# Modulation rows on GpSimd: 48 instead of 32 in each second-table stage, none in the sliding attention and the mixing stage

## The chip, the cores and the metric

The kernel runs on one core of a Trainium2 chip. The metric is the time of one execution on the device in microseconds (us). The engines are named as the profile names them: PE is TensorE (PEld its weight loads), DVE is VectorE, ACT is ScalarE, POOL is GpSimd, SP the engine whose queue issues nearly all loads here.

## What is computed

Three transformer-like layers on 256 tokens of width 1024, in float32. The first has gated linear attention, the second sliding-window attention with a shared key and value; each is followed by a retrieval over 16384 single-neuron experts. The third has retention beside latent attention (the mixing stage) and a mixture of 32 experts. Every norm is scaled and shifted by a modulation vector, and every residual is gated by one. These vectors depend only on the conditioning inputs `c` and `c_2`, not on the tokens, so their products can be computed at any time before they are used:

```python
mod = c_act @ mod_w[l] + mod_b[l]                       # D -> 6 D, also kv_mod and the third layer's
sh1, sc1, g1, sh2, sc2, g2 = jnp.split(mod, 6, axis=-1)
h = modulate(x, norm_g[l, 0], sh1, sc1)
x = x + (g1[:, None, :] * mixer(h)).astype(x.dtype)

def peer(h, w_q, subkeys, u_tab, v_tab):                # per head: two top-16, then the best 16 of 256 pairs
    u = u_tab[e]
    a = gelu(einsum('pd,phkd->phk', xb, u))
    return einsum('phk,phkd->pd', g * a, v_tab[e])
```

The kernel computes the retrieval densely: all 16384 rows of the first table (u) and then of the second (v), with a gate that is zero where an expert isn't chosen.

## The kernel before

**Modulation rows.** The modulation vectors have 160 blocks of 128 outputs; the weights of one block are a row of 512 KB in the stream, 128 partitions by 1024 values. The first 16 rows are made at the start. The other 144 go over GpSimd (`mod_pool`, L2499). For each row it waits for the load, multiplies the 1024 values by the activated conditioning (L2505), halves three times by addition (512, 256 and 128 columns: L2507, L2509, L2517) and leaves 128 partial sums per partition in a "part". TensorE then sums the part over the partitions with a matmul of one column (`column`, L773 and L775). Two buffers alternate: row j may be loaded when row j-2 is made (semaphore `mod_made`), and a part is written again when its column is done (`mod_column`).

**Where the rows lie.** `MODS_GLA` gives 40 rows to the first attention and the queries after it, `MODS_DOWN` 32 rows to each of the two second-table stages, `MODS_SWA` 16 to the sliding attention, `MODS_MIX` 16 to the mixing stage and `MODS_MOE` 8 to the last experts. In the sliding attention and the mixing stage the program of SP is written out by hand (`loads_with_mods`, L547): a list `at` says behind which weight slot a modulation load goes. It stands in the same queue as the loads of the ring of four weight slots, and waits there for `mod_made`. Groups of eight columns are taken by `mods_pe` (two groups after the sixth output projection, L1067; one after the retention values and one before the retention scores), and `mods_dve` adds the bias.

**The second-table stage.** `down_pe` (L954) runs over 128 tiles of the table, 16 in a turn of its loop. A tile is 12 matmuls of 512 columns (L973). ScalarE rounds the tile's two halves and the gated activations to their high parts (`down_high`, L1445 and L1453), VectorE subtracts to get the low parts (`down_low`, L2106 twice for the halves, L2109 for `a_parts`). Their program is in the order of tiles, and the order binds them: `a_parts` has two buffers, the table parts eight halves, that is four tiles. ScalarE waits at L1453 for TensorE's matmuls on the tile before last. SP loads eight tiles ahead (`v_used`: low parts of tile c-8 made; four ahead in the first turn). After every fourth table tile SP loads a modulation row into the first half of `hT` or into `mean`; on TensorE the column of a row stands behind tiles 3, 7, 11 and 15 of a turn. The parts lie in `hT`, four of them. All columns go to bank 0, and VectorE takes them together at the end (L2120).

**The sliding attention.** Four key tiles, four value slots, eight query tiles w_q0 to w_q7 (w_q0 and w_q1 as plain float32, L747; the others with weights split by ScalarE, L1292, and VectorE, L1746, L695 on TensorE). Behind w_q3 stand four small matmuls that rotate the keys (L1046), behind w_q7 eight for the queries (L1051). VectorE turns each with L2164, L2166 and L2168. Then come the scores, softmax, weighted values, and the output projection with the square sums of the next norm (L649).

**The mixing stage.** `mix_pe` begins with `ret_q`, `ret_k` (L695) and `ret_v` (L719), all with split weights; between the splits of `ret_k` and `ret_v` VectorE does one step of the rotation per slot (L2220, L2224).

## Time and profile before

| | us |
|---|---|
| median of 3 runs | 3214.8 |
| lowest and highest | 3210.15, 3217.36 |
| the profiled execution | 3215.8 |
| its span, first to last instruction | 3214.0 |

The granted TensorE clock over the profiled span was 0.965 of full speed.

| engine | busy us | share |
|---|---|---|
| PE | 2985.8 | 93% |
| PEld | 2696.5 | 84% |
| DVE | 2045.3 | 64% |
| ACT | 1621.4 | 50% |
| POOL | 1562.5 | 49% |

The two second-table stages run from 786 to 1154 us and from 1886 to 2255 us; the sliding attention follows the first, to about 1340 us, and the mixing stage the second, to about 2625 us. Busy shares over the whole span say little here, as the stages have different limits; each is read in its own window. A group of instructions that overlap is shown as one line with its count: "3.00 ... x2" is the time from the start of the first to the end of the second. An engine's idle time stands in brackets with what ended it.

### The profile page before, as it was taken

Reading aid. Unit: us, or ns where it says so; the run is one execution under the profiler, and the core shown is the slowest. Engines: PE = TensorE matmul, PEld = TensorE weight load, DVE = VectorE, ACT = ScalarE, POOL = GpSimd, SP = SyncE. Lnnn points to the kernel's source line nnn. Section 1 sums busy time; section 2 is a strip of 40 time slices with the busy share of each in tenths; the row PEclk is TensorE's granted clock in tenths of the full one; section 3 lists DMA queues with packets and bytes.
Section 4 is the critical chain, followed back from the end, with each engine's and each line's share of the span. In section 5 each row is a group of like instructions: output and inputs, shape, how many; then the busy total and the mean of one; then the engine's idle time right before and its main releaser. Section 6 shows DMA issues by size and latency. Waiting matters only on the chain.

```text
span 3214.0 us, 57845 instructions
## 1 busy us (share of the span) xinstructions
PE 2985.8 (93%) x18908; PEld 2696.5 (84%) x18908; DVE 2045.3 (64%) x3376; ACT 1621.4 (50%) x3195; POOL 1562.5 (49%) x1229
## 2 busy tenths in 40 slices
PE   7988999987999986999999789999799999999998
PEld 6678999976787875899999677778689789999997
DVE  6647960057888868279300778888784436777776
ACT  1124555578555543355555965555554325555553
POOL 5867898975444436158988645444361010000100
PEclk8989999999999997999999999999999999999998
DMA  6545555521766632345555037665464235555553
GB/s 246 201 148 175 181 181 181 183 72 59 261 230 228 228 134 105 109 159 182 182 182 189 7 131 257 226 229 202 151 216 145 92 125 191 190 194 191 197 194 125
DMA packets 153463, 552.57 MB, mean 172 GB/s; under 512 B 16896, under 2 KB 19712, under 8 KB 153232
## 3 DMA queue, kind: packets, MB, share of 16 engines
q1 hardware_dynamic: 151136, 547.42, 50.2%
q10 hardware_dynamic: 2224, 3.87, 0.4%
q8 instruction: 53, 0.87, 0.1%
q14 instruction: 50, 0.41, 0.0%
HBM read 550.17 MB, written 1.05 MB: 172 GB/s over the span
## 4 chain that ended last, share of the span: by engine, by line
PE 74%; ACT 9%; DVE 6%; issue 6%; POOL 3%; DMA 1%; ACTq 0%; DVEq 0%; SPq 0%; POOLq 0%
PE bank L947 23%; PE bank L973 20%; PE bank L1218 12%; PE bank L747 6%; PE bank L1239 5%; ACT hT L1434 5%; PE bank L695 3%; ACT hT L1430 2%; POOL arena L2505 1%; DVE w_parts L1746 1%; POOL arena L2507 1%; PE bank L649 1%; DMA arena<-stream 1%; POOL arena L2509 1%; DMA ring<-stream 1%
## 5 line engine op out<-in xcount | busy, mean ns | idle before, releaser
L2462 POOL TENSOR_TENSOR w_parts<-ring,w_parts 128x512 fp32r<-128x512 f32 x512 | 661.9, 1300 | 169.9 <-ACT w_parts L1399 119.3
L947 PE MATMUL bank<-h_parts,w_parts 128*128 128x256 f32 x6144 | 738.3, 283 | 5.1 <-POOL w_parts L2462 5.1
L947 PEld LDWEIGHTS bank<-h_parts,w_parts 128*128 128x128 f32 x6144 | 737.5, 191 | 5.5 <-POOL w_parts L2462 5.5
L2505 POOL TENSOR_TENSOR arena<-arena,cact 128x1024 f32<-128x1024 f32 x80 | 168.7, 2109 | 747.2 <-DMA arena<-stream 746.9
L1399 ACT ACTIVATE w_parts<-ring 128x512 fp32r<-128x512 f32 x512 | 322.8, 632 | 318.3 <-PE bank L947 316.4
L1218 PEld LDWEIGHTS bank<-h_parts,w_parts 128*128 128x128 f32 x3072 | 374.6, 193 | 3.8 <-DVE arena L2324 1.5
L1218 PE MATMUL bank<-h_parts,w_parts 128*128 128x256 f32 x3072 | 375.5, 284 | 1.4 <-DVE arena L2324 1.4
L1586 ACT ACTIVATE w_parts<-ring 128x512 fp32r<-128x512 f32 x384 | 241.9, 631 | 266.8 <-PE bank L1218 167.9
L973 PE MATMUL bank<-w_parts,a_parts 128*128 128x512 f32 x1536 | 371.0, 397 | 1.1 <-DVE a_parts L2109 1.1
L973 PE MATMUL bank<-h_parts,a_parts 128*128 128x512 f32 x1536 | 365.4, 393 | 6.1 <-DVE a_parts L2109 6.1
L2393 DVE TENSOR_TENSOR w_parts<-ring,w_parts 128x512 fp32r<-128x512 f32 x376 | 268.9, 727 | 150.3 <-ACT w_parts L1586 147.0
L973 PEld LDWEIGHTS bank<-h_parts,a_parts 128*128 128x128 f32 x1536 | 284.7, 188 | 80.4 <-DVE a_parts L2109 22.4
L973 PEld LDWEIGHTS bank<-w_parts,a_parts 128*128 128x128 f32 x1536 | 286.5, 190 | 60.7 <-DVE a_parts L2109 2.6
L1453 ACT ACTIVATE a_parts<-arena 128x256 fp32r (+1 forms) x256 | 107.1, 418 | 363.6 <-PE bank L973 361.7
L695 PE MATMUL bank<-h_parts,w_parts 128*128 128x256 f32 x1920 | 240.8, 287 | 16.5 <-DVE w_parts L1746 14.7
L695 PEld LDWEIGHTS bank<-h_parts,w_parts 128*128 128x128 f32 x1920 | 236.5, 195 | 20.4 <-issue 17.1
L2109 DVE TENSOR_TENSOR a_parts<-arena,a_parts 128x256 fp32r<-128x256 f32 x256 | 168.7, 659 | 115.6 <-ACT a_parts L1453 115.3
L1746 DVE TENSOR_TENSOR w_parts<-ring,w_parts 128x512 fp32r<-128x512 f32 x184 | 194.0, 1085 | 64.6 <-ACT w_parts L1292 63.2
L921 PE MATMUL bank<-hT,h_parts 128*128 128x128 f32 x1024 | 145.9, 295 | 68.8 <-ACT hT L1434 67.2
L2067 DVE COPY bank<-cst 128x128 f32<-128x128 f32 x2 | 0.6, 294 | 320.4 <-ACT arena L1404 320.4
L921 PEld LDWEIGHTS bank<-hT,h_parts 128*128 128x128 f32 x1024 | 129.1, 202 | 85.7 <-ACT hT L1434 85.6
L1239 PE MATMUL bank<-w_parts,a_parts 128*128 128x512 f32 x768 | 182.8, 394 | 4.9 <-DVE a_parts L2405 4.1
(325 smaller groups left out, 4595.0 us busy)
## 6 DMA issues: line engine op xcount, KB each, us to landing
ring<-stream SPq DMA_DIRECT2D x786, 512.0 KB, 3.4
arena<-stream SPq DMA_DIRECT2D x192, 512.0 KB, 4.3
hT<-stream SPq DMA_DIRECT2D x32, 512.0 KB, 4.6
mean<-stream SPq DMA_DIRECT2D x32, 512.0 KB, 4.5
arena<-consts ACTq DMA_DIRECT2D x1, 1536.0 KB, 6.3
xT<-xin ACTq DMA_DIRECT2D x1, 1024.0 KB, 10.7
out<-hT SPq DMA_DIRECT2D x4, 256.0 KB, 2.2
arena<-subk ACTq DMA_DIRECT2D x2, 128.0 KB, 2.1
```

The costliest lines, as they stand in the source:

```text
L695: mm = pe.matmul(t[:, 0:T], w[:, wp, q * P:(q + 1) * P], h_parts[:, hp, 4 * j + q, :], start=(j == 0 and q == 0 and i == 0), stop=(j == 1 ...
L921: mm = pe.matmul(bank[4 + k][:, (s % 4) * P:(s % 4 + 1) * P], hot2[:, s, :].bitcast(F32), hot1[:, s, :], start=True, stop=True)
L947: mm = pe.matmul(bank[k][:, 0:T], w[:, wp, ws], h_parts[:, hp, 4 * j + q, :], start=(j == 0 and q == 0 and i == 0), stop=(j == 1 and q == ...
L973: mm = pe.matmul(bank[4 + 2 * a + e][:, :], a_parts[:, k % 2, ap, a * P:(a + 1) * P], w[:, wp, :], start=False, stop=False, skip_group_che ...
L1218: mm = pe.matmul(bank[2 * e_par + m][:, f * T:(f + 1) * T], w[:, wp, q * P:(q + 1) * P], h_parts[:, hp, 4 * j + q, :], start=(j == 0 and q ...
L1239: mm = pe.matmul(bank[4 + 2 * a + e][:, :], a_parts[:, ap, f, a * P:(a + 1) * P], w[:, wp, :], start=(f == 0 and i == 0), stop=(f == 1 and ...
L1399: act.activation(w_parts[half % HALVES][:, 0, :], ring[slot_][:, j * 512:(j + 1) * 512], ACT.Copy).then_inc(sem(f"{n}_high"), 1)
L1586: act.activation(w_parts[half % HALVES][:, 0, :], ring[s][:, j * 512:(j + 1) * 512], ACT.Copy).then_inc(sem("e_high"), 1)
L1746: dve.tensor_tensor(w[:, 1, :], slot(name, k)[:, j * 512:(j + 1) * 512], w[:, 0, :].bitcast(F32), ALU.subtract).then_inc(sem("x_low"), 1)
L2393: dve.tensor_tensor(w[:, 1, :], ring[moe_slot(k)[0]][:, j * 512:(j + 1) * 512], w[:, 0, :].bitcast(F32), ALU.subtract).then_inc(sem("e_low ...
L2462: pool.tensor_tensor(w[:, 1, :], ring[(base + k) % RING][:, j * 512:(j + 1) * 512], w[:, 0, :].bitcast(F32), ALU.subtract).then_inc(sem(f" ...
L2505: pool.tensor_tensor(b3, b3, c_b, ALU.mult).then_inc(sem("mod_step"), 1)
```

## The change

The 16 rows of the sliding attention and the 16 of the mixing stage move into the two second-table stages, which get 48 each. Six rows go with a turn of 16 tiles, loaded and summed behind tiles 3, 6, 8, 11, 13 and 15 (`DOWN_AT`). The parts become six, two in each of three chunks of `hT`. The order of rows stays; since the rows of the second layer's stage begin at 104, GpSimd writes its first two turns out (the first eight rows use the first conditioning vector, the others the second) and loops over the rest. The SP programs of the sliding attention and the mixing stage become plain loops over weight slots. `mods_pe` and `mods_dve` are not called there any more.

```diff
-MODS_DOWN = ((56, 88), (104, 136))
-MODS_SWA = (88, 104)
-MODS_MIX = (136, 152)
+MODS_DOWN = ((56, 104), (104, 152))
+DOWN_AT = (3, 6, 8, 11, 13, 15)
+TURN_MODS = len(DOWN_AT)
...
-            return [hT[:, 4 + i, 0:P] for i in range(4)]
+            return [hT[:, 4 + i // 2, i % 2 * P:(i % 2 + 1) * P] for i in range(TURN_MODS)]
...
-                    if c % 4 == 3:
-                        mod_load(seg, seg[0] + c // 4)
+                    if c % 16 in DOWN_AT:
+                        mod_load(seg, seg[0] + c // 16 * TURN_MODS + DOWN_AT.index(c % 16))
...
-                        if c % 4 == 3:
-                            j = j0 + c // 4
-                            sp.wait_ge(sem("mod_made"), it * 4 + (j - 1))
-                            sp.dma_start(mod_buffers(seg)[j % 2], stream[it * 12 + (row0 + 3 * (c // 4))])\
+                        if c % 16 in DOWN_AT:
+                            i = c // 16 * TURN_MODS + DOWN_AT.index(c % 16)
+                            j = j0 + i
+                            sp.wait_ge(sem("mod_made"), it * TURN_MODS + (j - 1))
+                            sp.dma_start(mod_buffers(seg)[j % 2], stream[it * 3 * TURN_MODS + (row0 + 3 * i)])\
                               .then_inc(mod_landed[j % 2], 16)
...
-            at = [kv + 3 * i // 2 for i in range(10)] + [MO["swa_out"][0] + 2] * 4 + [MO["swa_out"][0] + 4, MO["swa_out"][0] + 5]
-            loads_with_mods(kv, MO["peer1_q"][0], MODS_SWA, MODS_SWA[0], at)
+            loads(kv, MO["peer1_q"][0])
...
-            loads_with_mods(mix, MO["mix_out"][1], MODS_MIX, MODS_MIX[0], [mix + 5 * i // 2 for i in range(16)])
+            loads(mix, MO["mix_out"][1])
...
-                    if k % 4 == 3:
-                        m = k // 4
-
-                        pe.wait_ge(sem("mod_made"), it * 4 + (mod_number(MODS_DOWN[l][0]) + m + 1))
-                        column(pe, bank[0][:, bass.ds(it * 4 + m, 1)], mod_parts(MODS_DOWN[l])[m]).then_inc(sem("mod_column"), 1)
+                    if k in DOWN_AT:
+                        m = DOWN_AT.index(k)
+
+                        pe.wait_ge(sem("mod_made"), it * TURN_MODS + (mod_number(MODS_DOWN[l][0]) + m + 1))
+                        column(pe, bank[0][:, bass.ds(it * TURN_MODS + m, 1)], mod_parts(MODS_DOWN[l])[m]).then_inc(sem("mod_column"), 1)
...
-            project_norm(pe, "swa_out", A.o, "w_out", "1b", between={5: lambda: [mods_pe(pe, MODS_SWA, g) for g in (11, 12)]})
+            project_norm(pe, "swa_out", A.o, "w_out", "1b")
...
-            mods_pe(pe, MODS_MIX, 17)
...
-            mods_pe(pe, MODS_MIX, 18)
...
-            for lo, hi, c in ((0, 2, c_b), (2, 8, c2_b if l else c_b)):
-                with pool.Fori(0, hi - lo) as it:
-                    for i in range(4):
-                        j = j0 + 4 * lo + i
-                        mod_pool(pool, seg, i, j, c, it)
+            turns = NK // 16
+            first = 2 if l else 0
+
+            for m in range(first * TURN_MODS):
+                mod_pool(pool, seg, m, j0 + m, c_b if m < 8 else c2_b)
+            with pool.Fori(0, turns - first) as it:
+                for i in range(TURN_MODS):
+                    mod_pool(pool, seg, i, j0 + first * TURN_MODS + i, c2_b if l else c_b, it)
...
-            mods_pool(pool, MODS_SWA, 0)
             peer_pool(pool, 1)
-            mods_pool(pool, MODS_MIX, 1)
```

## Rows read from the trace of the kernel before

**Rows 1.** The page, part 2: busy tenths of GpSimd in 40 slices.
```profile
POOL 5867898975444436158988645444361010000100
```

**Rows 2.** Chain that ended last, in second-table stages: start us, us, what.
```profile
799.70 0.11 PE bank L775 x2
...
810.95 11.02 PE bank L973 x48
...
1921.75 11.03 PE bank L973 x48
...
1957.60 11.22 PE bank L973 x48
...
2243.69 11.02 PE bank L973 x48
```

**Rows 3.** Stage window: length; PE, PEld, DVE, ACT, POOL busy; clock, DMA share, GB/s.
```profile
1957.60:2254.80 297.20, 294.70 (x1302) 238.25 (x1302) 250.89 (x307) 150.20 (x307) 130.34 (x100) 1.00 0.63 219
```

**Rows 4.** Timeline of GpSimd in second-table stages: start us, us, instruction, idle before.
```profile
786.62 1.90 POOL L2505 TENSOR_TENSOR hT<-hT,cact 128x1024 f32<-128x1024 f32 x1 [11.20 <-DMA hT<-stream]
...
790.84 0.46 POOL L2517 TENSOR_TENSOR hT<-hT 128x128 f32<-128x128 f32 x1 [0.17 <-POOL hT L2509]
...
1934.25 2.08 POOL L2505 TENSOR_TENSOR hT<-hT,cact 128x1024 f32<-128x1024 f32 x1 [5.11 <-DMA hT<-stream]
...
1940.92 2.09 POOL L2505 TENSOR_TENSOR mean<-mean,cact 128x1024 f32<-128x1024 f32 x1 [1.15 <-DMA mean<-stream]
```

**Rows 5.** Timeline of VectorE in second-table stages.
```profile
974.97 0.78 DVE L2109 TENSOR_TENSOR a_parts<-arena,a_parts 128x256 fp32r<-128x256 f32 x1 [1.26 <-ACT a_parts L1453]
...
978.52 0.68 DVE L2109 TENSOR_TENSOR a_parts<-arena,a_parts 128x256 fp32r<-128x256 f32 x1
...
1933.88 3.00 DVE L2106 TENSOR_TENSOR h_parts<-arena,h_parts 128x512 fp32r<-128x512 f32 x2
1936.80 1.51 DVE L2109 TENSOR_TENSOR a_parts<-arena,a_parts 128x256 fp32r<-128x256 f32 x1
...
1940.24 0.41 DVE L2109 TENSOR_TENSOR a_parts<-arena,a_parts 128x256 fp32r<-128x256 f32 x1
1940.58 2.98 DVE L2106 TENSOR_TENSOR w_parts<-ring,w_parts 128x512 fp32r<-128x512 f32 x2
...
1953.92 1.28 DVE L2106 TENSOR_TENSOR w_parts<-arena,w_parts 128x512 fp32r<-128x512 f32 x2
```

**Rows 6.** Timeline of SP's queue and of ScalarE in the sliding attention.
```profile
1207.72 0.33 SPq L545 DMA_DIRECT2D arena<-stream  x1
...
1212.49 0.63 ACT L1292 ACTIVATE w_parts<-ring 128x512 fp32r<-128x512 f32 x1 [4.77 <-DMA ring<-stream]
```

**Rows 7.** Timeline of TensorE in the sliding attention.
```profile
1197.88 7.07 PE L747 MATMUL bank<-arena,ring 128*128 128x256 f32 x32
...
1318.91 3.62 PE L747 MATMUL bank<-arena,ring 128*128 128x256 f32 x16
1322.36 1.84 PE L775 MATMUL bank<-cst,arena 128*128 128x1 f32 x16
...
1326.81 5.30 PE L747 MATMUL bank<-arena,ring 128*128 128x256 f32 x16
```

**Rows 8.** Timeline of VectorE in the sliding attention, a rotation's first and last step.
```profile
1257.81 0.42 DVE L2164 TENSOR_TENSOR arena<-bank,rope_s 128x256 f32<-128x256 f32 x1
...
1258.73 0.56 DVE L2168 TENSOR_TENSOR arena<-arena 128x256 f32<-128x256 f32 x1
```

**Rows 9.** Mixing stage: one window (columns as in rows 3), then TensorE's timeline.
```profile
2289.70:2365.10 75.40, 64.85 (x436) 58.48 (x434) 69.16 (x55) 34.72 (x62) 52.69 (x35) 1.00 0.65 218
...
2337.71 11.13 PE L719 MATMUL bank<-w_parts,h_parts 128*128 128x512 f32 x48 [0.93 <-DVE w_parts L1746]
...
2365.07 1.84 PE L775 MATMUL bank<-cst,arena 128*128 128x1 f32 x16
...
2367.03 42.04 PE L695 MATMUL bank<-h_parts,w_parts 128*128 128x256 f32 x336
```

## What the change should do to the time

> **What bounds the kernel now.** I read the page's slices first, then the second-table stages (786 to 1154 us and 1886 to 2255 us), then the two stages that lose work. [rows 1] are GpSimd's slices: 4 or 5 tenths in the two second-table stages (digits 11 to 14 and 25 to 28), and again right after each of them, in the sliding attention and in the mixing stage. In the second-table stage the chain of waits is nearly all matmuls of L973: 48 of them, four tiles, take 11.02 us, and 11.22 where something held them up [rows 2]. So a tile costs TensorE 2.755 us, and a modulation column 0.12 us (0.11 in the row at 799.70). From the group at 1957.60 to the end of the one at 2243.69 run 104 tiles in 297.1 us, which is 45.71 us for a turn of 16. Sixteen clean tiles and four columns would be 44.08 + 0.48 = 44.56, so four modulation rows now cost 1.15 us of stall a turn, 0.29 each.
>
> The stall comes from VectorE. It makes the low parts for the same tiles and is busy 250.9 of 297.2 us there [rows 3]. GpSimd needs 4.68 us for a modulation row while VectorE rests [rows 4]. While both work, VectorE's instructions stretch: a pair of 128x512 subtractions takes 3.00 us against 1.28, an a_parts subtraction 1.51 against 0.41 [rows 5]. Free, a tile costs VectorE 0.34 + 1.28 = 1.62 us. Between 1933.88 and 1953.92 three modulation rows follow each other while VectorE does six tiles, so two tiles take 6.68 us (6.70 from 1933.88 to 1940.58); so a modulation row takes 6.68 - 3.24 = 3.44 us from VectorE. TensorE wants two tiles in 5.57 us (with half a column each): VectorE falls back 1.1 us for each such row, and 0.29 of it shows as stall when it had no lag before. A tile without GpSimd gives back 2.755 - 1.62 = 1.14 us. The check: these three should cost 0.29 + 1.10 + 1.10 = 2.49 us; in the chain the eight tiles from 1932.90 (1921.75 + 11.03 + 0.12) to 1957.60 took 24.70 us against 22.28 clean, 2.42 us lost.
>
> **What the change takes away.** (a) Sliding attention. In the SP queue each modulation load waits for GpSimd, and the ring loads stand behind it: the one at 1207.72 goes out only then, and the ring load behind it lets ScalarE go on at 1212.49, after 4.77 us of idleness [rows 6]. TensorE has no gap until w_q0 and w_q1 are done at about 1205 (1197.88 + 7.07) [rows 7]. Without these loads the ring runs ahead, and six split projections (24 matmuls each, 3.0 us at the rate of 42.04 us for 336 [rows 9]) and four small rotations (an estimate of 1.2 us: 4 x 256 columns, and the waits for their banks) end near 1205 + 18.2 + 1.2 = 1224.5. Then VectorE's eight rotations follow; one takes 1.5 us where GpSimd does not touch it (1257.81 to 1259.30) [rows 8], so they end near 1237 instead of 1259.3: 22 us less. What is late next is TensorE with its projections; between 19 (their clock lower for part of it) and 24 us. (b) The two groups of columns inside the output projection, at 1322.36, hold TensorE for 2 x 1.96 = 3.9 us (1.96 is the group of the mixing stage, below), and the 16 matmuls after them take 5.30 instead of 3.62 us [rows 7]: 5.6 us in sum, 3.9 at least. VectorE's two small additions and the gains lie beside matmuls: nothing. (c) Mixing stage. From 2289.7 to 2365.1, 75.4 us, TensorE does 336 matmuls of 256 columns and 96 of 512. At the rates of stretches without idleness (42.04 us for 336, 11.13 for 48) that is 42.0 + 22.3 = 64.3 us, so 11.1 us are waits for VectorE, which is busy 69 of the 75 us [rows 9]. GpSimd's 35 instructions there are nearly nine modulation rows, 9 x 3.44 = 31 us of VectorE's 69; without them VectorE has 38 us of work in 64. I take 10 us, between 7 and 11. (d) The columns of the two groups there: 2365.07 to 2367.03, 1.96 us, and the same once more, 3.9 us. Sum of what goes: 22 + 5.6 + 10 + 3.9 = 41.5 us, from 33.8 to 44.5. The tiles opened later shift to other banks in the rotation of four; that costs nothing, since the order of openings and evictions stays.
>
> **What it adds.** In each second-table stage 16 more rows: 16 loads of 512 KB, 64 GpSimd instructions, 16 columns. The DMAs: the stage moves 219 GB/s now at a share of 0.63 [rows 3]; 22 loads instead of 20 per turn make that about 0.69, still far from full, so nothing for bandwidth. The wait for the row before last now stands more often in SP's queue; behind it are the table loads. These are issued eight tiles (22 us) ahead of VectorE, and a row needs up to 4.8 us to land [rows 6] and 5.5 us on GpSimd (1934.25 to 1939.77, where its idle time before 1940.92 begins) [rows 4], so the queue has over 10 us to lose first: nothing. TensorE's wait before a column looks for a row loaded some twelve tiles earlier: nothing. The unrolled GpSimd rows of the second layer issue the same instructions. What counts is VectorE's time. Its demand in a turn becomes 16 x 1.62 + 6 x 3.44 = 46.6 us, above TensorE's clean 44.80 (with six columns): VectorE becomes the bound.
>
> The order 3, 6, 8, 11, 13, 15 decides the rest. Rows at 3, 6 and 11 have a free tile before them; each leaves 1.1 - 0.29 = 0.81 us of lag, less than the 1.14 us that a free tile gives back. Rows at 8, 13 and 15 follow two tiles behind another and cost 1.10 each. A turn: 44.80 + 3 x 0.29 + 3 x 1.10 = 48.97 us, 3.26 more than now. Some rows begin while VectorE rests and take only 2.27 us from it (974.97 to 979.20, 4.23 us for work of 1.96) [rows 5]; of the eight in that stretch of 92 us this was one. With them I take +2.9 a turn for the six regular turns of a layer. The first turn has such rows mostly, +1.0. In the second the loads bunch, as they do now (the arena half of the ring opens at once): 0.29 + 5 x 1.10 = 5.8 us against about 2.8 now, +3.2 with the columns. A layer: 1.0 + 3.2 + 6 x 2.9 = 21.6; both: 43 us. Bounds: 0.29 for every row, 46.54 a turn, +0.83 x 16 = 13 us; and every turn as bunched as the second, 44.80 + 5.79 = 50.59, +4.9 x 16 = 78 us. I stay at 43 because both spots with contiguous rows show the full price.
>
> By the Trainium skill ("SBUF — State Buffer", section "Who interferes with whom") a VectorE instruction with two SBUF inputs and a GpSimd instruction that reads SBUF exclude each other for their whole length. The trace agrees in kind, not in full: a row that is 4.68 us long takes 3.44.
>
> **Sum.** The profiled execution has 3215.8 us (span 3214.0), 1.0 above the median of 3214.8. 3215.8 - 41.5 + 43 = 3217.3; for the median 3216.3, I say 3216. Within 0.2% (6.4 us, about what a measurement of this kernel can tell) this is no change: two large sums that cancel.
>
> **The rivals.** *Faster: the added rows hide.* If rows behind another also fall into VectorE's rests, each costs 0.29 and a turn 46.54: 13 us against 41.5, 3186; with half of them 3200. For it: the first turn of the first layer, where the chain shows groups of 11.02 in spite of its rows (810.95) [rows 2]. Against: VectorE has no rests while it lags. *Slower: GpSimd's rows run together in every turn.* Rows at 11, 13, 15 are loaded 5.6 us apart and GpSimd needs 5.5 us for one under contention. If the next row is there when one ends, VectorE never gets its free tile; the turn is 50.6 us, 78 - 41.5 = +36, 3251; if only some turns do so, 3235. It decides once a row waits in its buffer when GpSimd ends the one before, that is where GpSimd's 5.5 us exceed the spacing of the loads; for it the second turns, against it GpSimd's idle 1.15 us even between the contiguous rows [rows 4]. *Slower: the gain is smaller.* If in the attention and mixing stages ScalarE or a lower clock keeps half of the waits (a) and (c), 16 us stay: 3232. *Full exclusion.* If each row took its whole 4.68 us, two tiles would be 7.92 us, the lag per row 2.35, and a turn at least 44.80 + 14.1 - 4.6 = 54.3: +8.6 x 16 = 138, 3312. This is the skill's lock taken strictly; the triple speaks against it.
>
> **How the numbers follow.** Forecast 0.33 (3209 to 3222 on its own), hidden rows 0.28, run-together rows 0.28, smaller gain 0.09, full exclusion 0.02. Faster by over 0.2%: 0.29; within: 0.33; slower: 0.38. The range 3190 to 3246 leaves out the far half of the hidden case, the ends of the run-together case and full exclusion.
>
> **What would show it.** Right: second-table turns near 48.6 us, VectorE busy over 95% of them with little idleness before L2109, GpSimd rows in blocks of one, two and three; the sliding attention's last rotation 22 us earlier after the stage's start; no waits on L1746 in the mixing stage. Wrong: turns below 47 us or above 50; waits for ring loads left in the attention; VectorE's instructions stretched by clearly less than 3.4 us a row in a block.

## The result: 1.5% slower

The changed kernel takes 3259.4 us (median of 4, from 3252.6 to 3269.0), the kernel before 3212.7 beside it: 1.0146 times the time, 95% interval 1.0117 to 1.0175. The forecast of 3216 and its range up to 3246 were too low. The profiled executions took 3258.8 and 3215.8 us, 43.0 apart. One execution of the kernel of the first experiment ran at a granted clock of 0.456 and took 11133.6 us; it is left out of that kernel's numbers. By stages:

```
us                 first table  second table 1  attention  first table 2  second table 2  mixing   experts
before                 482.2        367.2         250.2        482.8          368.0        385.9    535.5
after                  482.4        414.7         220.0        483.3          411.4        366.2    535.1
forecast change          0          +21.6         -27.6          0            +21.6        -13.9      0
measured change        +0.2         +47.5         -30.2        +0.5           +43.4        -19.7    -0.4
```

(A second-table stage and the experts reach from their first matmul to the start of their last; "first table" from its first matmul to the first of the second table; "attention" and "mixing" from the start of the last matmul of a second-table stage to the first of the stage behind.) The saving was 49.9 us instead of 41.5, the cost 90.9 instead of 43. So the gain was found and somewhat larger, and the added rows cost twice what the sum gave them.

The page of the kernel after, GpSimd's, VectorE's and the clock's slices; the second is to be compared with [rows 1]:

```profile
DVE  6647950067998977379300889899664436777776
POOL 5867898865665530058988656565100001000100
PEclk8989999999999998999999999999999999999998
```

GpSimd stands at 5 or 6 tenths in the second-table stages and at 0 to 3 right behind them. The second-table stages in two windows (columns: length; PE, PEld, DVE, ACT, POOL busy; clock, DMA share, GB/s), to compare with [rows 3]:

```profile
787.70:1202.80 415.10, 380.03 (x1634) 303.15 (x1633) 362.29 (x376) 183.82 (x376) 251.44 (x192) 0.98 0.63 221
1905.70:2317.50 411.80, 376.77 (x1633) 301.55 (x1633) 360.25 (x376) 183.71 (x376) 250.40 (x192) 0.99 0.63 222
```

VectorE is busy 87% of the time, not over 95%: it isn't simply full, and it isn't the bound that the forecast made it. Yet TensorE waits for it. The waits in the second of these windows, after (line, what it waited for, us in total, times, longest), then the same stage of the kernel before:

```profile
PE bank L963 <- DVE a_parts L2097: 34.8, 39, 1.8
...
DVE a_parts L2097 <- ACT a_parts L1441: 47.9, 46, 6.2
```

```profile
PE bank L973 <- DVE a_parts L2109: 4.2, 8, 0.9
...
DVE a_parts L2109 <- ACT a_parts L1453: 57.6, 65, 6.2
```

TensorE waits 34.8 us for VectorE (4.2 before), and in the same stage VectorE idles 47.9 us for ScalarE's high parts, which in turn wait until TensorE frees one of the two a_parts buffers. Both happen in turns: VectorE falls back while GpSimd works, catches up, and can't get more than the two buffers ahead.

One regular turn shows it. GpSimd's timeline, the product that begins each row, with its idle time before:

```profile
2103.79 1.90 POOL L2491 TENSOR_TENSOR hT<-hT,cact 128x1024 f32<-128x1024 f32 x1 [8.86 <-DMA hT<-stream]
...
2114.55 2.12 POOL L2491 TENSOR_TENSOR mean<-mean,cact 128x1024 f32<-128x1024 f32 x1 [5.41 <-DMA mean<-stream]
...
2120.08 2.08 POOL L2491 TENSOR_TENSOR hT<-hT,cact 128x1024 f32<-128x1024 f32 x1
...
2130.68 1.90 POOL L2491 TENSOR_TENSOR mean<-mean,cact 128x1024 f32<-128x1024 f32 x1 [5.09 <-DMA mean<-stream]
...
2136.00 2.08 POOL L2491 TENSOR_TENSOR hT<-hT,cact 128x1024 f32<-128x1024 f32 x1
...
2141.47 2.35 POOL L2491 TENSOR_TENSOR mean<-mean,cact 128x1024 f32<-128x1024 f32 x1
```

These are blocks of one, two and three rows, as the forecast had them, but inside a block there is no idle time at all, where [rows 4] had 1.15 us. So it is in 9 of the 12 regular turns: the second row of the pair and both followers in the block of three begin within 0.12 us of the row ahead. VectorE's timeline in the same stretch:

```profile
2129.06 0.43 DVE L2097 TENSOR_TENSOR a_parts<-arena,a_parts 128x256 fp32r<-128x256 f32 x1 [0.78 <-ACT a_parts L1441]
...
2132.03 0.83 DVE L2097 TENSOR_TENSOR a_parts<-arena,a_parts 128x256 fp32r<-128x256 f32 x1 [1.27 <-ACT a_parts L1441]
...
2136.24 4.08 DVE L2094 TENSOR_TENSOR w_parts<-arena,w_parts 128x512 fp32r<-128x512 f32 x2
...
2147.71 0.41 DVE L2097 TENSOR_TENSOR a_parts<-arena,a_parts 128x256 fp32r<-128x256 f32 x1
```

and TensorE's, with the idle time before:

```profile
2103.09 5.97 PE L963 MATMUL bank<-w_parts,a_parts 128*128 128x512 f32 x24
...
2109.48 5.74 PE L963 MATMUL bank<-h_parts,a_parts 128*128 128x512 f32 x24 [0.29 <-DVE a_parts L2097]
...
2120.74 2.88 PE L963 MATMUL bank<-h_parts,a_parts 128*128 128x512 f32 x12
2125.33 3.04 PE L963 MATMUL bank<-h_parts,a_parts 128*128 128x512 f32 x12 [1.70 <-DVE a_parts L2097]
...
2136.76 2.99 PE L963 MATMUL bank<-h_parts,a_parts 128*128 128x512 f32 x12
2141.24 3.02 PE L963 MATMUL bank<-w_parts,a_parts 128*128 128x512 f32 x12 [1.49 <-DVE a_parts L2097]
...
2145.83 3.02 PE L963 MATMUL bank<-w_parts,a_parts 128*128 128x512 f32 x12 [1.46 <-DVE a_parts L2097]
```

VectorE stands idle 0.78 and 1.27 us just ahead of the block of three; then its pair of subtractions takes 4.08 us where 1.28 is the free time, and TensorE waits 1.49 and 1.46 us. From 2132.03 to 2147.71, both the start of an a_parts subtraction, VectorE does four tiles in 15.68 us; TensorE alone needs 11.02.

What each block costs TensorE in this turn can be read from the starts of its tiles, with 2.755 us for a tile and 0.16 for a column, the measured price of one (below). The single row: 6.39 us from 2103.09 to 2109.48 for two tiles and a column, 0.7 lost. The pair: 4.59 us from 2120.74 to 2125.33 for one tile, 1.8 lost. The block of three: 9.07 us from 2136.76 to 2145.83 for two tiles and a column, 3.4 lost. In sum 5.9 us.

Now the stages that lost work. In VectorE's timeline the last rotation of the sliding attention begins 80.3 us after the stage did (1202.8); in [rows 8] it was 104.1 (from 1153.7):

```profile
1283.12 0.42 DVE L2152 TENSOR_TENSOR arena<-bank,rope_s 128x256 f32<-128x256 f32 x1
```

TensorE's output projection has eight pieces of 16 matmuls. After, the first three stand in one row, then the sixth and the eighth (to compare with [rows 7]):

```profile
1325.44 10.60 PE L737 MATMUL bank<-arena,ring 128*128 128x256 f32 x48 [0.57 <-issue]
...
1344.08 3.62 PE L737 MATMUL bank<-arena,ring 128*128 128x256 f32 x16
...
1351.85 3.62 PE L737 MATMUL bank<-arena,ring 128*128 128x256 f32 x16
```

The first three and the eighth before:

```profile
1300.27 10.60 PE L747 MATMUL bank<-arena,ring 128*128 128x256 f32 x48 [0.57 <-issue]
...
1332.39 3.62 PE L747 MATMUL bank<-arena,ring 128*128 128x256 f32 x16
```

And a window of the mixing stage, to compare with [rows 9]:

```profile
2352.71:2455.12 102.41, 102.41 (x769) 98.66 (x769) 63.48 (x86) 60.70 (x107) 0.00 (x0) 1.00 0.55 185
```

In the mixing window TensorE has no gap in 102.41 us; it does 336 + 96 + 336 matmuls there (40.59, 21.95 and 40.47 us in the timeline).

### The profile page after: what moved, and what is told of

Its sections match the earlier page's. It is cut to its first block, busy times and chain, and to the rows that moved or that the text cites. A ratio compares the mean times of both kernels' runs of the same rounds, so it can differ in the third digit from the quotient of the medians.

```text
span 3257.0 us, 58401 instructions
## 1 busy us (share of the span) xinstructions
PE 2991.1 (92%) x18900; PEld 2695.8 (83%) x18900; DVE 2084.7 (64%) x3372; ACT 1621.2 (50%) x3195; POOL 1553.8 (48%) x1229
## 4 chain that ended last, share of the span: by engine, by line
PE 60%; issue 15%; DVE 8%; ACT 8%; POOL 8%; DMA 1%; DVEq 0%; ACTq 0%; POOLq 0%; SPq 0%
PE bank L937 23%; PE bank L1206 11%; PE bank L963 7%; PE bank L1227 5%; PE bank L737 5%; ACT hT L1422 5%; PE bank L685 4%; DVE h_parts L2094 2%; DVE a_parts L2097 2%; DVE w_parts L2094 2%; ACT hT L1418 2%; POOL mean L2491 1%; POOL hT L2491 1%; POOL mean L2493 1%; POOL arena L2491 1%
## 5 line engine op out<-in xcount | busy, mean ns | idle before, releaser
L2446 POOL TENSOR_TENSOR w_parts<-ring,w_parts 128x512 fp32r<-128x512 f32 x512 | 659.7, 1299 | 327.0 <-ACT w_parts L1387 286.1
L963 PE MATMUL bank<-w_parts,a_parts 128*128 128x512 f32 x1536 | 383.3, 404 | 35.3 <-DVE a_parts L2097 35.3
L963 PE MATMUL bank<-h_parts,a_parts 128*128 128x512 f32 x1536 | 376.1, 398 | 34.8 <-DVE a_parts L2097 34.5
L2491 POOL TENSOR_TENSOR arena<-arena,cact 128x1024 f32<-128x1024 f32 x48 | 99.0, 2063 | 566.3 <-DMA arena<-stream 566.2
L2377 DVE TENSOR_TENSOR w_parts<-ring,w_parts 128x512 fp32r<-128x512 f32 x376 | 271.1, 732 | 148.8 <-ACT w_parts L1574 145.5
L2097 DVE TENSOR_TENSOR a_parts<-arena,a_parts 128x256 fp32r<-128x256 f32 x256 | 215.1, 840 | 96.2 <-ACT a_parts L1441 96.1
L1734 DVE TENSOR_TENSOR w_parts<-ring,w_parts 128x512 fp32r<-128x512 f32 x184 | 145.6, 806 | 95.2 <-ACT w_parts L1280 93.7
L2479 POOL TENSOR_TENSOR w_parts<-ring,w_parts 128x512 fp32r<-128x512 f32 x8 | 12.2, 1536 | 381.8 <-ACT w_parts L1574 381.7
```

Source lines behind the costliest of these rows:

```text
L963: mm = pe.matmul(bank[4 + 2 * a + e][:, :], a_parts[:, k % 2, ap, a * P:(a + 1) * P], w[:, wp, :], start=False, stop=False, skip_group_che ...
L2097: dve.tensor_tensor(a_parts[:, k % 2, 1, :], W[:, bass.ds(it * 16 + k, 1), :].rearrange("p i t -> p (i t)"), a_parts[:, k % 2, 0, :].bitca ...
L2377: dve.tensor_tensor(w[:, 1, :], ring[moe_slot(k)[0]][:, j * 512:(j + 1) * 512], w[:, 0, :].bitcast(F32), ALU.subtract).then_inc(sem("e_low ...
L2446: pool.tensor_tensor(w[:, 1, :], ring[(base + k) % RING][:, j * 512:(j + 1) * 512], w[:, 0, :].bitcast(F32), ALU.subtract).then_inc(sem(f" ...
L2491: pool.tensor_tensor(b3, b3, c_b, ALU.mult).then_inc(sem("mod_step"), 1)
```

## The experiments

Every theory below is about one of three things: whether the two sums are independent, what a row on GpSimd takes from VectorE and TensorE, and how this depends on the distance between rows. "Turn" is 16 tiles, measured between every sixteenth a_parts subtraction of VectorE; where one number stands for regular turns it is the mean of turns 3 to 7 of both layers.

### The saving alone

No row in the sliding attention and the mixing stage, and none added elsewhere.

```diff
-MODS_DOWN = ((56, 104), (104, 152))
-DOWN_AT = (3, 6, 8, 11, 13, 15)
+MODS_DOWN = ((56, 88), (104, 136))
+DOWN_AT = (3, 7, 11, 15)
```

> The kernel after with 32 rows in each second-table stage again (behind tiles 3, 7, 11 and 15); the other 32 rows are left out altogether, so their modulation vectors are the bias alone. It prices what leaves the sliding attention and the mixing stage, without what is added elsewhere. In the profiles of before and after, the first of these stages is 30 us shorter (249.8 to 219.6) and the second 20 us (385.4 to 365.8). If the two halves of the change are independent: 3213 - 50 = 3163 us, second-table stages near 368 us each as before. If part of the shorter stages comes from the other half of the change (a later start, another clock): above 3170 us.

Measured: 3163.7 us (median of three), 0.9843 times the kernel before (0.9822 to 0.9863). Attention 218.7, mixing 365.5, second-table stages 368.4 and 368.2 us, the regular turn 45.67. The saving stands by itself, is 50 us, and doesn't touch the second-table stages; what the change costs is all in them.

### The added rows without their arithmetic

The changed kernel; in the second-table stages a row's load, its waits, its last small sum and its column stay, and nothing else of it.

```diff
+            if seg in MODS_DOWN:
+                pool.sem_inc(sem("mod_step"), 3)
+            else:
                 pool.tensor_tensor(b3, b3, c_b, ALU.mult).then_inc(sem("mod_step"), 1)
                 pool.wait_ge(sem("mod_step"), step(1))
                 pool.tensor_tensor(buf[:, 0:512], buf[:, 0:512], buf[:, 512:1024], ALU.add).then_inc(sem("mod_step"), 1)
                 pool.wait_ge(sem("mod_step"), step(2))
                 pool.tensor_tensor(buf[:, 0:256], buf[:, 0:256], buf[:, 256:512], ALU.add).then_inc(sem("mod_step"), 1)
                 pool.wait_ge(sem("mod_step"), step(3))
```

> The kernel after, but in the second-table stages GpSimd does only the last addition of each modulation row (128 columns); the multiplication and the first two additions are left out, all loads, waits and columns stay. Theory, VectorE loses its time to GpSimd's instructions: a turn of 16 tiles falls from about 51 to 45 us, the stages from 415 and 412 to about 365, the kernel to about 3165 us. Rival, the additional loads or the longer SP queue cost the time: the stages stay near 410 and the kernel near 3255 us.

Measured: one execution, 3156.6 us, stages 362.1 and 361.5 us; every turn behind the first takes 45.04 us. The first stage in a window:

```profile
787.00:1150.00 363.00, 363.00 (x1632) 300.70 (x1631) 216.84 (x378) 184.01 (x376) 27.61 (x48) 0.99 0.71 253
```

TensorE has no gap, at 253 GB/s. Loads and waits in SP's queue cost nothing, columns nothing but their own time: those steps of the forecast were right (its clean turn with six columns, 44.80, was 0.24 short; six columns in 45.04 - 44.08 us make 0.16 each). VectorE's busy time falls to 216.8 of 363 us, 216 per stage, against 361 with 48 full rows and 305 with 32: (361 - 216) / 48 = 3.0 us and (305 - 216) / 32 = 2.8 us of VectorE for each row. The 3.44 us of the forecast was, if anything, too much. So the price of a row on VectorE isn't the failed step either.

### Small loads

The changed kernel; each of its second-table row loads brings only 64 of 512 KB.

```diff
-                sp.dma_start(mod_buffers(seg)[j % 2], stream[mod_row(m)]).then_inc(mod_landed[j % 2], 16)
+                if seg in MODS_DOWN:
+                    sp.dma_start(mod_buffers(seg)[j % 2][:, 0:P], stream[mod_row(m)][:, 0:P]).then_inc(mod_landed[j % 2], 16)
...
```

> The kernel after, but each modulation row of the second-table stages loads only 128 of its 1024 columns (64 KB instead of 512 KB); GpSimd clears the rest of the two buffers once per stage and does all its instructions. Left out is so most of each row's sum. Theory, VectorE loses its time to GpSimd: no change, 3250 to 3262 us, turns near 51 us. Rival, bandwidth or late table loads: the stages fall towards 370 us, the kernel towards 3175.

Measured: one execution, 3244.4 us, stages 403.3 and 409.2 us against 414.7 and 411.4. The smaller loads take back 13.6 us of the 90.9, so the DMAs' own traffic isn't what costs most. These 13.6 us can come from the time of landing, which moves the rows' starts (3.0 and 3.8 us from issue in the median for the two buffers, against 4.5 and 5.3), or from the traffic; this run doesn't separate the two.

### The same number of rows, closer together

As the saving alone (32 rows per stage, the same 32 left out), but the four rows of a turn lie two tiles apart instead of four.

```diff
-DOWN_AT = (3, 7, 11, 15)
+DOWN_AT = (3, 5, 7, 9)
```

> Leaves out the same 32 modulation rows as the run of the saving alone, so 32 rows per second-table stage; but the four rows of a turn are loaded and summed behind tiles 3, 5, 7 and 9 in place of 3, 7, 11 and 15. Nothing else differs. Theory A (a row with enough free tiles behind it costs 0.25 to 0.3 us, a row that follows another with no gap 1.10): a turn of 16 tiles takes 44.8 + 0.3 + 3 x 1.1 = 48.4 us instead of 45.8, the stage 385 to 391 us instead of 368, the kernel 3200 to 3212 us instead of 3165.7. Theory B (the number of rows sets the cost): stage 368 us, kernel 3166 us.

Measured: one execution, 3228.6 us; the stages take 397.7 and 397.8 us instead of 368.4 and 368.2, the regular turn 49.68 instead of 45.67. Not one row was added, and it costs 29.5 us a stage. The number of rows alone doesn't set the cost; at a given number their distance does. It is even more than expected: (49.68 - 44.80) / 4 = 1.22 us a row. TensorE's waits of the second stage:

```profile
PE bank L963 <- DVE a_parts L2097: 25.5, 25, 1.9
```

Two windows of the first stage, where the granted clock falls behind a stretch in which TensorE waited:

```profile
852.00:860.00 8.00, 5.93 (x26) 4.45 (x25) 8.00 (x7) 3.20 (x7) 7.45 (x7) 1.00 0.64 250
860.00:868.00 8.00, 7.97 (x29) 6.46 (x30) 4.70 (x8) 1.95 (x5) 0.31 (x1) 0.79 0.60 200
```

In the ten regular turns such stretches make about 0.9 us a turn on average, if the time lost is counted as the length times one less the granted clock; so at most 0.9 of the 4.9 us beyond the clean turn are the clock, and at least 1.0 of the 1.22 us a row stays without it.

GpSimd's products in one turn:

```profile
2082.12 1.90 POOL L2492 TENSOR_TENSOR mean<-mean,cact 128x1024 f32<-128x1024 f32 x1 [2.70 <-DMA mean<-stream]
2087.56 2.22 POOL L2492 TENSOR_TENSOR hT<-hT,cact 128x1024 f32<-128x1024 f32 x1
2095.65 2.04 POOL L2492 TENSOR_TENSOR mean<-mean,cact 128x1024 f32<-128x1024 f32 x1 [2.46 <-DMA mean<-stream]
2123.41 1.90 POOL L2492 TENSOR_TENSOR hT<-hT,cact 128x1024 f32<-128x1024 f32 x1 [22.26 <-DMA hT<-stream]
```

The 22 us of rest behind the rows don't pay back what was lost among them.

### Half a row

The changed kernel with 48 rows per stage; of each second-table row the product and the last sum stay.

```diff
+            if seg in MODS_DOWN:
+                pool.sem_inc(sem("mod_step"), 2)
+            else:
                 pool.tensor_tensor(buf[:, 0:512], buf[:, 0:512], buf[:, 512:1024], ALU.add).then_inc(sem("mod_step"), 1)
                 pool.wait_ge(sem("mod_step"), step(2))
                 pool.tensor_tensor(buf[:, 0:256], buf[:, 0:256], buf[:, 256:512], ALU.add).then_inc(sem("mod_step"), 1)
                 pool.wait_ge(sem("mod_step"), step(3))
```

> The changed kernel with 48 rows per second-table stage; of each row's four GpSimd instructions in those stages only the product (1.90 us while VectorE rests) and the last sum (0.45 us) are done, half of the time of 4.68 us. So a row takes at most about half of 3.3 us from VectorE, and the rows can't run together. Theory A (two buffers of a_parts let VectorE fall back by some 1.3 us at no cost, beyond that it is stall): the turn is 45.0 to 45.8 us, the stage 362 to 368 us, the kernel 3158 to 3170 us. Theory B (the cost is in proportion to GpSimd's time on VectorE's memory): half of the 6.4 us of a turn beyond 45.04, turn 48.2 us, stage 388 us, kernel 3205 us.

Measured: one execution, 3159.3 us, stages 363.9 and 362.5 us, regular turn 45.2. The first stage:

```profile
787.00:1150.00 363.00, 362.91 (x1626) 299.58 (x1626) 287.36 (x376) 183.97 (x376) 133.69 (x96) 0.99 0.73 253
```

VectorE loses (287.4 - 216.8) / 48 = 1.47 us to each of these rows, half of the full price, and TensorE loses next to nothing: 1 to 2 us a stage. Half the disturbance costs not half of 50 us but almost zero. The loss behaves like a threshold: what the two a_parts buffers and the free tiles cover is free, and only what is beyond shows. (The half rows also never touch: the shortest idle time ahead of one is 0.38 us. So this run halves a row's price and removes the blocks at once.)

### GpSimd held to TensorE's pace

The changed kernel, complete; GpSimd begins a row only when TensorE has freed the a_parts of a given tile, so rows begin 3, 3, 2, 3, 3 and 2 tiles apart.

```diff
+PACE = (-3, 0, 3, 5, 8, 11)
...
                 for i in range(TURN_MODS):
+                    pool.wait_ge(sem(f"{n}_parts_free"), it * 32 + (first * 32 + DHALVES + 2 * PACE[i]))
                     mod_pool(pool, seg, i, j0 + first * TURN_MODS + i, c2_b if l else c_b, it)
```

> The changed kernel, and GpSimd begins each modulation row of a second-table stage only when TensorE has come to a given tile (tiles 3, 3, 2, 3, 3 and 2 apart), so that no three rows run with no gap. Theory A (the bunching of three rows costs the 2 us of a turn beyond 48.6): the turn of 16 tiles falls from 51.3 to about 48.5 us, the stage to 390 us, the kernel to 3210 to 3225 us. Theory B (each added row costs the same wherever it lies): no change, stage 413 us and kernel 3255 to 3265 us. If the wait makes rows late for their columns the stage is longer than 413 us.

Measured: one execution, 3228.2 us, stages 400.9 and 401.2. The regular turn is 49.63 us, the same to 0.01 us in ten turns, instead of 51.3. TensorE's waits in the second stage:

```profile
PE bank L964 <- DVE a_parts L2098: 21.6, 26, 1.8
```

Three of GpSimd's products, each released by TensorE:

```profile
1022.04 1.90 POOL L2494 TENSOR_TENSOR mean<-mean,cact 128x1024 f32<-128x1024 f32 x1 [3.43 <-PE bank L964]
1027.83 2.20 POOL L2494 TENSOR_TENSOR hT<-hT,cact 128x1024 f32<-128x1024 f32 x1 [0.44 <-PE bank L964]
1037.86 1.90 POOL L2494 TENSOR_TENSOR mean<-mean,cact 128x1024 f32<-128x1024 f32 x1 [4.40 <-PE bank L964]
```

A wait on the disturbing engine gives back 31 us, 24.0 of them in the second-table stages (3.4 of the others lie ahead of the first table, where the kernels don't differ). The bunching was real, but removing it doesn't bring the turn to 48.5. TensorE's timeline shows where the rest is lost:

```profile
1024.66 6.09 PE L964 MATMUL bank<-w_parts,a_parts 128*128 128x512 f32 x24
...
1032.04 5.74 PE L964 MATMUL bank<-h_parts,a_parts 128*128 128x512 f32 x24 [1.17 <-DVE a_parts L2098]
```

From 1024.66 to 1032.04 two tiles and a column take 7.38 us, 1.7 more than clean, while the row at 1027.83 follows the one at 1022.04 two tiles behind; the turn's other pair two tiles apart loses 1.8 in the same way (1049.29 to 1056.75). These two pairs make 3.5 of the turn's 4.6 us beyond 45.04, so here too it is mostly the rows two tiles apart that cost.

### Rows at more even distances

The changed kernel, complete, with the loads at distances 3, 3, 2, 3, 2, 3. The last load ahead of the first table's end moves to another ring slot, so one wait moves with it.

```diff
-DOWN_AT = (3, 6, 8, 11, 13, 15)
+DOWN_AT = (2, 5, 8, 10, 13, 15)
...
-                    if c == RING - 1:
+                    if c == RING - 2:
```

> The changed kernel with the row loads behind tiles 2, 5, 8, 10, 13 and 15 of 16, so distances 3, 3, 2, 3, 2, 3 in place of 3, 2, 3, 2, 2, 4. Theory A (rows close together cost most): the turn falls by the part that the pair of short distances in a row costs, to 49.5 to 50.5 us, stage 398 to 406 us, kernel 3230 to 3247 us. Theory B (each row costs the same): 3255 to 3262 us.

Measured: one execution, 3245.0 us, stages 405.8 and 405.5, regular turn 50.2 us. A few us from the order of six numbers, and less than from pacing, since the loads still follow VectorE's uneven pace.

### Five rows a turn

Leaves out 16 rows (8 of the 48 in each stage); the others go ten to 32 tiles, in loops of 32, no two closer than three.

```diff
-MODS_DOWN = ((56, 104), (104, 152))
-DOWN_AT = (3, 6, 8, 11, 13, 15)
+MODS_DOWN = ((56, 96), (104, 144))
+DOWN_AT = (3, 6, 9, 12, 15, 19, 22, 25, 28, 31)
```

> Leaves out 8 of the 48 modulation rows of each second-table stage (their values are the bias alone); the other 40 go five to 16 tiles of the table, their loads behind tiles 3, 6, 9, 12, 15, 19, 22, 25, 28 and 31 of 32, so that each load is three or four tiles behind the one before and each row has a tile of the table without a row beside it. The stage took 368 us with 32 rows and 413 us with 48. Theory A (it is the rows two tiles apart that cost: a row of 5.5 us behind another with no gap drives VectorE two tiles back, more than its two buffers cover): the stage takes 369 to 378 us, under 1 us per added row, and the kernel 3165 to 3190 us. Theory B (each added row costs the same, 45 us by 16 rows = 2.8 us, wherever it lies): the stage takes 390 us and the kernel 3210 us.

Measured: one execution, 3204.8 us, stages 390.4 and 381.7: neither theory. With 44.92 for a clean turn, the regular turn of 47.82 is 0.58 us a row, between the 0.25 of rows four apart and the 1.10 that the forecast gave to rows two apart. The two layers differ by 9 us with the same instructions. In the first, two rows of the regular turns begin with no gap behind the row ahead, in the second none does (closest 0.42 us); that small shifts of the rows decide here is likely, not shown.

All regular turns together:

```
kernel                      rows  closest distances     turn us   per row over the clean turn, us
four apart (before)           4   4, 4, 4, 4             45.80     0.25
half rows                     6   as after               45.21     0.03
five                          5   3 and 4                47.82     0.58
paced                         6   3, 3, 2, 3, 3, 2       49.63     0.77
even                          6   3, 3, 2, 3, 2, 3       50.20     0.86
after                         6   3, 2, 3, 2, 2, 4       51.32     1.05
bunched                       4   2, 2, 2, then 10       49.68     1.22
```

(The clean turn is 45.04 with six columns, as measured without arithmetic, less 0.12 for each column fewer, as the forecast counted them; before: (45.80 - 44.80) / 4. "Bunched" holds up to 0.2 us a row of lower clock.)

### The 32 rows placed elsewhere, three times

The kernel before, complete, with its 32 rows of the attention and mixing stages moved within these stages, to keep them away from the rotations. If what the change saved was only the rows' bad places, it can be had without the added rows. First try:

```diff
-            at = [kv + 3 * i // 2 for i in range(10)] + [MO["swa_out"][0] + 2] * 4 + [MO["swa_out"][0] + 4, MO["swa_out"][0] + 5]
+            at = [kv, kv + 2, kv + 4] + [so + 3] * 10 + [so + 4, so + 4, so + 5]
...
-            loads_with_mods(mix, MO["mix_out"][1], MODS_MIX, MODS_MIX[0], [mix + 5 * i // 2 for i in range(16)])
+            loads_with_mods(mix, MO["mix_out"][1], MODS_MIX, MODS_MIX[0], [MO["mla_cq"][0] + 1 + 25 * i // 16 for i in range(16)])
```

> The kernel before with its 32, 16 and 16 rows, but placed where no one waits for what they hold up: in the sliding attention three rows early, ten behind the fourth output slot, three later; in the mixing stage from the latent queries on, where VectorE has no rotation steps, the first group of columns taken after the retention gates. Theory, the cost of the rows there is the place (the ring loads behind them in the SP queue, VectorE's rotations beside them): the attention loses about 15 of its 30 us, the mixing stage 10 to 15 of its 20, the kernel about 3185 us. Rival, the rows cost the same wherever they lie in these stages: 3210 us.

Measured: 3237.0 us, 1.007 times (1.0053 to 1.0086): slower than before. Attention 267.3 us, mixing 390.0. SP's queue:

```profile
1275.24 40.93 SPq L545 DMA_DIRECT2D arena<-stream  x10
```

and TensorE:

```profile
1320.60 5.64 PE L748 MATMUL bank<-arena,ring 128*128 128x256 f32 x16 [31.52 <-DMA ring<-stream]
```

The ring load of piece 3 waits for piece 0's first matmul; the ten row loads behind it go out one by one as GpSimd frees a buffer, for 40.9 us, and piece 4's weights stand behind them: 31.5 us of TensorE. The output projection itself began earlier (1274.16 against 1300.27), so the attention part of the idea stood; the queue took it back. Second try, one load earlier, and in the mixing stage two rows first and fourteen with the gates:

```diff
-            at = [kv, kv + 2, kv + 4] + [so + 3] * 10 + [so + 4, so + 4, so + 5]
+            at = [kv, kv + 2, kv + 4] + [so + 2] * 11 + [so + 3] * 2
...
-  [MO["mla_cq"][0] + 1 + 25 * i // 16 for i in range(16)]
+  [mix, mix + 2] + [mix + 21 + 2 * i for i in range(14)]
```

> The kernel before with the same 32 rows per second-table stage, its 16 + 16 other rows placed elsewhere: in the sliding attention three rows with the first projections and the rest behind the load of output piece 2 (one before the load that waits for that projection itself), in the mixing stage two at the start and fourteen with the gate projections, their arithmetic behind the rotations. The stages with 32 rows stay at 368 us. If what the change saved was the rotations, that GpSimd ran 22 us late, and TensorE's waits for the mixing rows, most of it comes without any added row: sliding attention 225 to 235 us (250 before, 220 with no rows), mixing stage 370 to 378 us (386 before, 366 with no rows), kernel 3178 to 3195 us. If the loads behind one another again hold the ring of weights, it is 3210 us or above.

Measured: 3193.0 us, 0.9939 times (0.9922 to 0.9955), attention 237.4, mixing 377.6, second-table stages 367.0 and 366.0. The fastest complete kernel here, with no row moved to another stage. VectorE's softmax scalings stretch beside GpSimd's rows, first and last group of eight:

```profile
1262.60 6.55 DVE L2158 TENSOR_SCALAR arena<-arena 128x128 f32<-128x128 f32 x8
...
1278.70 1.93 DVE L2158 TENSOR_SCALAR arena<-arena 128x128 f32<-128x128 f32 x8
```

Eight scalings take 6.55 us while GpSimd works and 1.93 when it has stopped. The rows weren't kept away from the rotations, though: the load of output piece 2 goes out early, and four of the eleven rows behind it run from 1224.49 to 1244.0, beside the eight rotations. These take 20.2 us (1222.79 to 1242.95), where the changed kernel, without rows there, needs 11.0 (1273.48 to 1284.50). The third try spreads the later rows so that they lie behind the scalings:

```diff
-            at = [kv, kv + 2, kv + 4] + [so + 2] * 11 + [so + 3] * 2
+            at = [kv, kv + 2, kv + 4] + [so + 2] * 7 + [so + 3] * 2 + [so + 4] * 2 + [so + 5] * 2
```

> As the better placement before it, with the 13 later rows of the sliding attention spread: seven behind the load of output piece 2, two behind each of pieces 3, 4 and 5. VectorE's last 16 scalings in the softmax took 12.6 us beside GpSimd's rows and 3.9 us without them. If that is all, the sliding attention falls from 237 to about 229 us and the kernel from 3193 to 3185 us. If the rows of pieces 3 to 5 hold the ring (each pair waits for GpSimd, 5 us a row against 3.5 us a piece), the output projection waits 10 us or more and it is 3195 to 3205 us.

Measured: 3204.4 us, 0.9968 times (0.9955 to 0.9982), attention 246.4: worse than the second try. The scalings are fast now (1.93 us for eight), but the output projection begins 132.6 us after the stage's start, 132.5 in the second try (122.6 in the changed kernel). The rotations, still beside four rows, ended 1.8 us later in the stage than in the second try, so the fast scalings gave back about that much, not the 8 us expected. Nor is it the ring, which held TensorE 0.34 us only. What makes it worse is the column of a row:

```profile
1321.58 3.57 PE L776 MATMUL bank<-cst,arena 128*128 128x1 f32 x16 [7.91 <-POOL arena L2518]
```

TensorE waits 7.9 us behind piece 5, in the second group of columns, for a row that GpSimd had begun at 1316.96, at 4.5 us a row without a gap. The expectation had asked for the ring alone and forgotten who reads the rows.

## Why the prediction was wrong, step by step

**The sliding attention, 22 + 5.6: right.** The last rotation came 23.8 us earlier in its stage, and the output projection began 24.0 us earlier (146.6 us after the stage's start before, 122.6 after). From the sixth piece to the eighth it is 7.77 us instead of 13.48: 5.7. Together 29.7 of the 30.2 measured.

**The mixing stage, 10 + 3.9: under-sized.** It gave 19.7. The waits went, all of them, and the columns too. The rest is the rate that the sum took as clean: 336 matmuls in 42.04 us [rows 9] were themselves among GpSimd's rows; without them they take 40.59 and 40.47, and 96 of 512 columns take 21.95 where the sum had 22.3. The forecast compared a disturbed stretch with another one that was only less disturbed.

**DMAs and SP's queue at nothing: right** (the run without arithmetic).

**VectorE's price for a row, 3.44 us: right in kind, a little high.** Measured 3.0 per row. By the Trainium skill ("SBUF — State Buffer", section "Who interferes with whom") the two engines exclude each other for whole instructions on their shared port. As an estimate from this rule, a row of 4.68 us would cost all of it. The runs show about two thirds, 3.0 for a full row and 1.47 for half of one, as the forecast said against the strict reading.

**The regular turn, +2.9: this step failed.** It measured 51.32 us on average against 45.80, +5.5. The failed sentence is "Rows at 8, 13 and 15 follow two tiles behind another and cost 1.10 each", with the one ahead of it, that a free tile gives back 1.14 us. The 1.10 was read where GpSimd idled 1.15 us between rows [rows 4], and in that gap VectorE ran at its free pace. Without the gap four tiles and three rows took 15.68 us (rows shown above). TensorE needs 11.02 for four tiles and 0.3 for their columns, so VectorE falls back 15.68 - 11.3 = 4.4, over three 1.45 us a row, not 1.10, although a row takes less of VectorE's time than the sum had ((15.68 - 6.48) / 3 = 3.07 us): three rows now lie within four of VectorE's tiles, 1.3 for each, where the sum gave two to each. A gap of a single microsecond was in the price and went away with the change.

On TensorE's side, in the turn shown: the block of three lost 3.4 us where the sum had 0.29 + 1.10 + 1.10 = 2.49, the pair 1.8 instead of 1.39, the single row 0.7 instead of 0.29. Together 5.9 instead of 4.17; the average turn lies 51.32 - 45.04 = 6.3 above the clean one. So every price of the sum was too low, the block's most. The other two parts of the 2.7 us that the turn had beyond the forecast's 48.6 are small: 0.24 for the columns, and 0.36 that the sum took off for rows in VectorE's rests. What the trace of before showed of a regular turn was four tiles apart only.

"VectorE becomes the bound" failed as well: at 3.0 us a row its demand in a turn is 16 x 1.62 + 6 x 3.0 = 43.9 us, below TensorE's 45.04, and it was busy 87%. It is late in each block and idle between them. Nor is the clock the reason in these turns: it was 0.99 of full speed from 888 to 1200 us and 1.00 from 2010 to 2315.

**Why the gap went.** A row's load goes out when VectorE has used the ring slot, so the loads follow VectorE's pace, not TensorE's. VectorE falls back under a row and then does its tiles in 1.6 us each; the loads bunch in that stretch. SP's queue, the three row loads ahead of the block of three:

```profile
2125.16 0.33 SPq L582 DMA_DIRECT2D mean<-stream  x1
...
2129.05 0.33 SPq L582 DMA_DIRECT2D hT<-stream  x1
...
2136.47 0.33 SPq L582 DMA_DIRECT2D mean<-stream  x1
```

The first two go out 3.9 us apart, where two tiles of TensorE are 5.6. The second row's weights wait in their buffer, and the third's load goes out 0.4 us after its buffer's row was made (2136.03); it has landed when GpSimd ends the second row. This the forecast had as a rival ("run together in every turn", 0.28), priced at 50.6 for the turn and 3251, and it argued against it with the 1.15 us. It was the case, though not as told there: VectorE does get free tiles (rests of 5 to 9 us of GpSimd in the turn shown), but it can't use them, because it can't be more than two a_parts buffers ahead. Against the paced kernel the bunching itself is 51.32 - 49.63 = 1.7 us a turn, 13.8 us in the first stage and 10.2 in the second; the kernel of 32 rows placed close shows the same from the other side. So the bunching is a part of the failure; the price of two rows two tiles apart, which pacing doesn't remove, is the other.

**The first two turns, +1.0 and +3.2: under-sized.** They took 52.05 and 55.58 us against 48.57 and 47.03 in the first layer, +12.0 together, and +12.9 in the second. The second turn holds a block of five rows with no gap inside; and the clock fell: 0.94 over this turn in both layers, 1.00 before, which is 3.4 us of the turn's length. Two neighbouring stretches of it after (columns as above):

```profile
840.00:848.00 8.00, 6.89 (x29) 4.92 (x28) 8.00 (x6) 3.56 (x8) 7.51 (x7) 1.00 1.02 401
848.00:856.00 8.00, 6.78 (x23) 5.45 (x24) 8.00 (x8) 2.38 (x5) 7.53 (x7) 0.79 0.78 279
```

TensorE had been busy 6.9 of the 8 us ahead; the granted clock then is 0.79 on average, so part of the stretch ran at 1.2 GHz, and once more from 864 to 872. In the first layer of the paced kernel the clock stays at 1.00 there and the turn is 52.55. Waiting had a second price here, which no term of the sum held.

The sum once more with what was measured: 24.9 for the four early turns and 66.0 for the twelve regular ones make 90.9, less 49.9 is +41.0; the remaining 2 us of 43.0 lie in the stages that the change doesn't touch, most of them (1.4) ahead of the first table. What stays open is what the 13.6 us of the small loads are, why five rows a turn cost 0.66 us each in the first layer and 0.51 in the second, and what deeper a_parts buffers would give, which wasn't tried. That the two a_parts buffers are the limit rests on the waits shown (VectorE for ScalarE, ScalarE for TensorE) and not on a run that changed their number.

## What to carry to other kernels

When an engine disturbs another that feeds the critical one through a shallow buffer, the cost of one more disturbance is not a price times a count: read how far apart the disturbances are, what the buffer covers (here 1.5 us of VectorE's time per row was free, and 3.0 wasn't), and reprice the closest pair without the gap that it has now. A rate taken as clean should come from a stretch in which the disturbing engine is idle. And before rows are moved to another stage, move them within their own: the better place there gave 20 us, where the move cost 47 (by the medians).

## What the runs showed of the hardware that was not expected

- Half of the GpSimd work per row (1.90 + 0.45 us) cost TensorE 0.03 us; the whole (4.68 us) cost 0.25 us at four tiles' distance and 1.22 at two. GpSimd's product itself grew from 1.90 to at most 2.45 us under contention, so most of the loss is on VectorE's side, whose pair of 1.28 us went up to 4.08.
- The granted clock fell to 0.79 of full speed over 8 us behind stretches in which TensorE was busy 5.9 to 6.9 of 8 us, though not behind all of them: in the paced kernel it stayed at 1.00 behind one with 5.73. In that kernel's regular turns, with the waits spread evenly, it was 1.00 throughout.
- 253 GB/s with a DMA share of 0.71 over a whole stage left TensorE busy 363.00 of 363.00 us.
